# One phase for all rounded matmul operands: the second class of SBUF start addresses is given up

## The chip, the cores and the metric

The kernel runs on one core of one Trainium2 chip. The metric is the device time of one execution in microseconds (us); the figure of a kernel is the median of its runs. The core's engines are TensorE (matmuls, "PE" in the profile, with its weight loads shown apart as "PEld"), VectorE (DVE), ScalarE (ACT), GpSimd (POOL), and SyncE, from whose queue (SPq) nearly all transfers from HBM are issued. Every operand of a matmul lies in SBUF: 128 partitions, with one byte address per tensor that is the same in all partitions. This case is about that address, taken modulo 512.

## The reference, cut to what matters

Two blocks of two layers each work on 256 tokens of width 2048, in float32. The first block is a state-space layer and a latent-attention layer, each with a layer norm behind it; the second is a gated MLP and a stick-breaking attention layer, with RMS norms. Nearly all arithmetic is in products of activations with weight matrices that are read once from HBM:

```
x = ssd_mixer:  x @ w_in (2048 x 10304) -> conv, chunked scan, gate, norm -> @ w_out (4096 x 2048)
x = dsa_mixer:  x @ w_in (2048 x 4944) -> c_q, c_kv, index, gate
                c_q @ w_uq, @ w_idx_q; per head k = w_uk c_kv, v = c_kv w_uv, softmax over the chosen keys
                (o * silu(gate)) @ w_out (4096 x 2048)
h = gmlp:       xn @ w_in (2048 x 12288) -> gelu, rms norm, token mixing, gate -> @ w_out (4096 x 2048)
h = stick:      xn @ w_in (2048 x 8192) -> q, k, v, gate; stick-breaking attention -> @ w_out (2048 x 2048)
out = rms_norm(h, final_g)
```

## The kernel before, in words

**Rounded operands in two halves.** A float32 matrix is split into a head, rounded to the type fp32r, and a rest, which is the matrix less its head, rounded again. A product of two matrices is then three matmuls in fp32r: head by head, head by rest, rest by head. ScalarE makes the head of a weight unit (`e.copy(wh, RAW)`, line 1125), VectorE its rest (line 1546), and TensorE reads both. The activations are kept in the same form: `AA` holds the transposed input of a layer (16 blocks of 128 rows, head and rest, 256 tokens each), `YY` the input of an output projection (32 such blocks), `CQ` and `CK` the normed low-rank queries and keys.

**Units and slots.** The weights come in 822 units of up to 128 x 1024 float32 (512 KB), in an order written out by `Plan`. Each unit is transferred into one of four `RAW` buffers, then cast and subtracted into a slot that holds head and rest, 8 KB in each partition. There are always three slots (`W0` to `W2`), and more where a stage leaves room: `WY24` and `WY28` inside `YY`, `Wx7`, and the spares `WA`, `WB`, `WC` around the output projections. `Plan.slots` assigns them; addresses play no part in it.

**Which operand moves.** A matmul has a stationary operand of 128 columns, loaded by a LDWEIGHTS of its own, and a moving operand that is streamed. In most blocks the weight is stationary and the activations move, 256 columns at a time. In the blocks of `TOKENS` (the output projections o1 to o4, and cq, v5, v7) the activation is stationary and the weight moves: 256 columns at a time in o1 to o4, 512 in the others. The profile's names give the moving operand first: `G<-AA,W` of shape 128x256 is AA streamed past a stationary weight unit, `G<-W,AA` of shape 128x512 is a weight unit streamed past a stationary piece of AA. All these matmuls are issued at line 703, and each has a weight load of its own.

**Where the operands lie.** Two constants give the start address modulo 512 of each rounded buffer:

```python
STILL, MOVING = 128, 496
LINES = {"CQ": MOVING, "CK": MOVING, "Wx7": STILL, "SPH": MOVING, "SPL": MOVING, "TGR": STILL, "ONR": STILL}
```

`place` (line 237 on) rounds an address up to the given phase. Each of the three main slots has two views, 368 bytes apart, in one piece of memory; `pair_of` takes the view `W3M` at phase 496 for units of o1 to o4, and `W3` at phase 128 for all others (names `W0m` and `W0` in the profile):

```python
        W3.append(place(f"W{i}", [P, 2 * UW], R, line=STILL))
        W3M.append(place(f"W{i}m", [P, 2 * UW], R, top[0] - 8 * UW + MOVING - STILL))
        top[0] += MOVING - STILL
    AA = place("AA", [P, 16, 2, T], R, line=MOVING)
```

`YY` with `WY24` and `WY28` and the copy `AS` of AA that v5 and v7 read as stationary for most of their units (made by SyncE's `copy_in`) lie at 128; the spares `WA`, `WB`, `WC` (function `spare`) at 496; `CQ`, `CK`, `SPH`, `SPL` at 496; `Wx7`, `TGR`, `ONR` at 128. All parts of these tensors that a matmul reads start a multiple of 512 bytes further on, so the phase of a tensor is the phase of each of its operands. Float32 tensors, used by the small matmuls and transposes between, are placed at multiples of 64 bytes with no phase of their own.

**Order of the work.** Each engine has its own program, written out in the same walk over the blocks (`walk`). The TensorE program runs a unit of matmuls, then one step of each active side task (transposes, scores, sums over partitions: tiles named `M<-...`), then the next unit. A unit waits for its rest (`rest`), a slot's next cast waits for the last matmul that reads the slot.

Of the kernel before, what the change touches and what calls it, by code (L numbers as in the profile page):

```python
# [19 lines left out]
NEG = -1.0e30  # L20
SCALE = 128.0 ** -0.5
SPANS = ((0, P), (P, 384))
STILL, MOVING = 128, 496
LINES = {"CQ": MOVING, "CK": MOVING, "Wx7": STILL, "SPH": MOVING, "SPL": MOVING, "TGR": STILL, "ONR": STILL}
GATES = ((1, 2), (3,), (4,), (5,), (6,), (7,), (), ())
LAST_COLS = ((0, 512), (512, 512), (1024, 512), (1536, 256), (1792, 256))
# [2397 lines left out]
```

How the kernel before makes its waits and increments, by code:

```python
        def fetch(u):  # L561
            s = u % NR
            if u >= NR:
                e.wait_ge(*on("rest", u - NR))
            for a0, nk, width, o, cn, src in units[u][3]:
                dst = RAW[:, s, a0:a0 + nk * width].rearrange("p (k n) -> p k n", k=nk)[:, :, o:o + cn]
                e.dma_start(dst, src).then_inc(*landed(raw_here[s], "raw", u))
            fetched[0] = u + 1
# [22 lines left out]
        def dt_task():  # L591
            for _ in range(8):
                yield
            e.wait_ge(*on("dt", "cs"))
            e.dma_start(cs_d[:, :], YT[0:64, 1, :]).then_inc(*landed(d["cs_stored"], "csd"))
            yield
# [1 line left out]
        def ssd(g):  # L598
            for _ in range(6):
                yield
            if g == 0:
                e.wait_ge(*on("csd"))
                e.wait_ge(*on("conv", ("bc", 0), 0, 3))
            else:
                e.wait_ge(*on("decay", g - 1, 1))
            e.dma_start(CSB[:, :, :], cs_d[8 * g:8 * g + 8, :].rearrange("h t -> (h t)").partition_broadcast(P)
                        ).then_inc(*landed(d["cs_landed"], "cs", g))
            yield
# [1 line left out]
        def ev_ms():  # L610
            e.wait_ge(*on("kw"))
            e.wait_ge(*on("end2", "act"))
            e.dma_start(KI[0:64, :], KW[0:64, :]).then_inc(*landed(d["ki_landed"], "ki"))
            e.dma_start(KI[64:128, :], KW[0:64, :]).then_inc(*landed(d["ki_landed"], "ki"))
            yield
# [34 lines left out]
        def copy_in(s):  # L650
            e.wait_ge(*done(("o2" if s == 1 else "o3", 4)))
            for h in range(2):
```

## Time and profile before

| | |
|---|---|
| median of 3 runs | 2435.77 us (2435.55 to 2437.74) |
| the profiled execution, span | 2435.7 us, 45481 instructions |
| PE busy | 2423.8 us (100%), 19626 matmuls |
| weight loads (PEld) busy | 2341.2 us (96%) |
| DVE / ACT / POOL busy | 1571.2 (65%) / 1243.2 (51%) / 90.5 us (4%) |
| HBM | 452.18 MB read, 187 GB/s over the span |

The span is the time from the first to the last instruction of the profiled execution. The profile gives no other time for that execution; its span is 0.07 us under the median of the runs. A matmul's own duration (some 275 ns for 256 columns) is longer than the distance between two starts, since matmuls are pipelined: the pace of the stream is read from the starts, that is from the first column of the timeline and the counts behind it. "Busy" is the union of the overlapping durations.

### The profile page before, as it was taken

The numbers are of one execution on the slowest core, as the hardware profiler recorded it, in microseconds if no ns is written. First come the engines' busy times: TensorE is split into PE (matmuls) and PEld (weight loads), VectorE is DVE, ScalarE is ACT, GpSimd is POOL, SyncE is SP. The second block draws the span as 40 slices with busy tenths as digits, with TensorE's granted clock in tenths as the row PEclk, the third lists the DMA queues.
The fourth block names the chain that finished last, engine by engine and source line by source line (L and its number), as shares of the span: only waits on it lengthen the run. The fifth ranks groups of instructions, "written<-read, shape, count | busy, mean of one in ns | idle before, by whom it ended". The sixth has DMA issues, their size and how long they took to land.

```text
span 2435.7 us, 45481 instructions
## 1 busy us (share of the span) xinstructions
PE 2423.8 (100%) x19626; PEld 2341.2 (96%) x19626; DVE 1571.2 (65%) x2109; ACT 1243.2 (51%) x1426; POOL 90.5 (4%) x68
## 2 busy tenths in 40 slices
PE   9999999999999999999999999999999999999998
PEld 9999999999999999999988899999999999999998
DVE  6778878866577776666575555655655555555556
ACT  5445665554454565554464444544544445455453
POOL 0001000110021000000000000000000000000002
PEclk9999999999999999999999999999999999999999
DMA  7665656657755645546757666666555576555645
GB/s 238 198 196 180 210 180 187 185 174 236 232 175 174 199 150 165 152 150 231 232 185 244 190 203 198 187 186 197 180 190 186 190 233 208 184 171 178 188 161 182
DMA packets 267434, 467.93 MB, mean 192 GB/s; under 512 B 18955, under 2 KB 70497, under 8 KB 265313
## 3 DMA queue, kind: packets, MB, share of 16 engines
q1 hardware_dynamic: 267233, 465.02, 60.9%
q8 instruction: 155, 2.54, 0.4%
q14 instruction: 46, 0.38, 0.1%
HBM read 452.18 MB, written 4.26 MB: 187 GB/s over the span
## 4 chain that ended last, share of the span: by engine, by line
PE 98%; DVE 1%; ACT 0%; issue 0%; DMA 0%; SPq 0%; ACTq 0%
PE G L703 91%; PE M L703 5%; PE M L716 1%; DMA RAW<-in_ssd_w_in 0%; DVE W2m L1546 0%; DVE W0m L1546 0%; DVE E L1639 0%; ACT W0m L1125 0%; DVE E L1680 0%; DVE SZ L1708 0%; DVE E L1641 0%; ACT L1205 0%; DVE W L1546 0%; DVE W1m L1546 0%; ACT YY L1131 0%
## 5 line engine op out<-in xcount | busy, mean ns | idle before, releaser
L703 PE MATMUL G<-AA,W 128*128 128x256 f32 x7908 | 942.6, 277 | 1.1 <-DVE W L1546 1.0
L703 PEld LDWEIGHTS G<-AA,W 128*128 128x128 f32 x7908 | 917.9, 188 | 7.3 <-issue 4.1
L1546 DVE TENSOR_TENSOR W<-RAW,W 128x1024 fp32r<-128x1024 f32 x446 | 557.4, 1251 | 370.6 <-ACT W L1125 369.4
L1125 ACT CAST W<-RAW 128x1024 fp32r<-128x1024 f32 x446 | 464.8, 1047 | 467.7 <-PE G L703 457.8
L703 PE MATMUL G<-AA,WY 128*128 128x256 f32 x2508 | 305.3, 278 | 0.0
L703 PEld LDWEIGHTS G<-AA,WY 128*128 128x128 f32 x2508 | 293.2, 188 | 2.5 <-issue 2.2
L1546 DVE TENSOR_TENSOR WY<-RAW,WY 128x1024 fp32r<-128x1024 f32 (+1 forms) x112 | 140.8, 1259 | 74.9 <-ACT WY L1125 74.9
L703 PE MATMUL G<-W0m,YY 128*128 128x256 f32 x1512 | 183.8, 276 | 1.0 <-DVE W0m L1546 1.0
L703 PE MATMUL G<-W1m,YY 128*128 128x256 f32 x1512 | 182.9, 276 | 0.1
L703 PE MATMUL G<-W,YY 128*128 128x512 f32 x792 | 181.3, 389 | 0.0
L703 PE MATMUL G<-W2m,YY 128*128 128x256 f32 x1488 | 180.5, 276 | 0.0
L703 PEld LDWEIGHTS G<-W0m,YY 128*128 128x128 f32 x1512 | 176.9, 188 | 1.8 <-DVE W0m L1546 1.5
L703 PEld LDWEIGHTS G<-W,YY 128*128 128x128 f32 x792 | 148.4, 188 | 30.8
L703 PEld LDWEIGHTS G<-W1m,YY 128*128 128x128 f32 x1512 | 176.6, 188 | 0.5 <-DVE W1m L1546 0.3
L703 PEld LDWEIGHTS G<-W2m,YY 128*128 128x128 f32 x1488 | 174.0, 188 | 0.4 <-issue 0.2
L1125 ACT CAST WY<-RAW 128x1024 fp32r<-128x1024 f32 (+1 forms) x112 | 116.2, 1043 | 101.2 <-PE G L703 100.1
L1546 DVE TENSOR_TENSOR W1m<-RAW,W1m 128x1024 fp32r<-128x1024 f32 x63 | 77.2, 1225 | 74.3 <-ACT W1m L1125 74.2
L1546 DVE TENSOR_TENSOR W0m<-RAW,W0m 128x1024 fp32r<-128x1024 f32 x63 | 78.4, 1244 | 68.4 <-ACT W0m L1125 68.3
L1546 DVE TENSOR_TENSOR W2m<-RAW,W2m 128x1024 fp32r<-128x1024 f32 x62 | 76.9, 1241 | 67.7 <-ACT W2m L1125 67.4
L1125 ACT CAST W0m<-RAW 128x1024 fp32r<-128x1024 f32 x63 | 66.2, 1051 | 80.8 <-PE G L703 80.7
L1125 ACT CAST W1m<-RAW 128x1024 fp32r<-128x1024 f32 x63 | 66.1, 1050 | 80.5 <-PE G L703 78.1
L1125 ACT CAST W2m<-RAW 128x1024 fp32r<-128x1024 f32 x62 | 65.2, 1052 | 79.6 <-PE G L703 78.3
(306 smaller groups left out, 2398.0 us busy)
## 6 DMA issues: line engine op xcount, KB each, us to landing
RAW<-in_a_w_in SPq DMA_DIRECT2D x192, 512.0 KB, 3.8
RAW<-in_ssd_w_in SPq DMA_DIRECT2D x160, 512.0 KB, 4.4
RAW<-in_b_w_in SPq DMA_DIRECT2D x128, 512.0 KB, 4.1
RAW<-in_dsa_w_in SPq DMA_DIRECT2D x72, 512.0 KB, 3.6
RAW<-in_ssd_w_out SPq DMA_DIRECT2D x64, 512.0 KB, 4.6
RAW<-in_dsa_w_out SPq DMA_DIRECT2D x64, 512.0 KB, 4.1
RAW<-in_a_w_out SPq DMA_DIRECT2D x64, 512.0 KB, 3.6
RAW<-in_b_w_out SPq DMA_DIRECT2D x32, 512.0 KB, 3.7
```

The lines of the kernel that those rows point to most:

```text
L703: return e.matmul(o, l, r, start=start, stop=stop, skip_group_check=True)
L716: return e.transpose(o, i, idn)
L1125: e.copy(wh[:, 0:n], RAW[:, v % NR, 0:n]).then_inc(*up(cast_done, "cast", v))
L1546: e.tensor_tensor(wl[:, 0:n], RAW[:, v % NR, 0:n], wh[:, 0:n].bitcast(F), ALU.subtract).then_inc(*up(rest_done, "rest", v))
```

## The change

Both constants become 128. Nothing else in the code is edited.

```diff
--- before.py
+++ after.py
@@ -20,7 +20,7 @@
-STILL, MOVING = 128, 496
+STILL, MOVING = 128, 128
 LINES = {"CQ": MOVING, "CK": MOVING, "Wx7": STILL, "SPH": MOVING, "SPL": MOVING, "TGR": STILL, "ONR": STILL}
```

What follows from it: `AA`, `CQ`, `CK`, `SPH`, `SPL`, the spares and the units of o1 to o4 in the main slots start at phase 128. The two views `W3` and `W3M` of a slot fall together. The slots lose the 368 bytes between the views, so AA starts 1392 bytes lower, and the small float32 tensors behind it (`ident`, `ones` and so on) move down with it, by 1408 bytes. YY and what is laid out behind it keep their phases; the float32 tensors behind `CK` and `CQ` in the attention stage change theirs by 128 bytes. The instructions, their number, their order, the units, the slots, the transfers and all waits stay as they are.

## Rows read from the trace of the kernel before

**Rows 1.** The page, part 1, and the granted clock in 40 slices.

```profile
PE 2423.8 (100%) x19626; PEld 2341.2 (96%) x19626; DVE 1571.2 (65%) x2109; ACT 1243.2 (51%) x1426; POOL 90.5 (4%) x68
PEclk9999999999999999999999999999999999999999
```

**Rows 2.** The page, part 4: the chain of work that ended last.

```profile
PE 98%; DVE 1%; ACT 0%; issue 0%; DMA 0%; SPq 0%; ACTq 0%
```

**Rows 3.** Groups by shape, PE: the twelve rounded groups of 256 moving columns, less one.

```profile
L703 PE MATMUL G<-AA,W 128*128 128x256 f32 x7908 | 942.6, 277 | 1.1 <-DVE W L1546 1.0
L703 PE MATMUL G<-AA,WY 128*128 128x256 f32 x2508 | 305.3, 278 | 0.0
L703 PE MATMUL G<-W0m,YY 128*128 128x256 f32 x1512 | 183.8, 276 | 1.0 <-DVE W0m L1546 1.0
L703 PE MATMUL G<-W1m,YY 128*128 128x256 f32 x1512 | 182.9, 276 | 0.1
L703 PE MATMUL G<-W2m,YY 128*128 128x256 f32 x1488 | 180.5, 276 | 0.0
L703 PE MATMUL G<-AA,Wx 128*128 128x256 f32 x528 | 63.9, 276 | 0.0
L703 PE MATMUL G<-CQ,W 128*128 128x256 f32 x456 | 54.3, 277 | 0.0
L703 PE MATMUL G<-WA,YY 128*128 128x256 f32 x408 | 47.7, 275 | 0.0
L703 PE MATMUL G<-WB,YY 128*128 128x256 f32 x408 | 47.6, 275 | 0.0
L703 PE MATMUL G<-CK,W 128*128 128x256 f32 x192 | 23.6, 278 | 0.0
L703 PE MATMUL G<-WC,YY 128*128 128x256 f32 x48 | 5.9, 275 | 0.0
```

**Rows 4.** The same view: groups of 512 moving columns with the stationary operand at 496.

```profile
L703 PE MATMUL G<-W,AA 128*128 128x512 f32 x240 | 57.0, 394 | 0.0
L703 PE MATMUL G<-WY,CK 128*128 128x512 f32 x72 | 18.2, 401 | 0.0
L703 PE MATMUL G<-WB,AA 128*128 128x512 f32 x60 | 15.6, 403 | 0.0
L703 PE MATMUL G<-WA,AA 128*128 128x512 f32 x60 | 15.6, 403 | 0.0
L703 PE MATMUL G<-W,CK 128*128 128x512 f32 x24 | 6.1, 400 | 0.0
```

**Rows 5.** Timeline of PE, 2030 to 2047 us: start, duration, operands, count (moving 496, stationary 128).

```profile
2036.67 2.88 PE L703 MATMUL G<-AA,Wx 128*128 128x256 f32 x24
2039.39 5.60 PE L703 MATMUL G<-AA,W 128*128 128x256 f32 x48
```

**Rows 6.** Timeline of PE, 2108 to 2122 us (512 columns, moving 128, stationary 128).

```profile
2108.49 2.88 PE L703 MATMUL G<-Wx,YY 128*128 128x512 f32 x12
2111.21 8.32 PE L703 MATMUL G<-W,YY 128*128 128x512 f32 x36
```

**Rows 7.** Timeline of PE, 696 to 713 us (AA at 496 as stationary).

```profile
697.00 8.56 PE L703 MATMUL G<-W,AA 128*128 128x512 f32 x36
705.40 2.94 PE L703 MATMUL G<-WA,AA 128*128 128x512 f32 x12
708.17 4.32 PE L703 MATMUL G<-AA,W 128*128 128x256 f32 x36
712.33 0.93 PE L716 MATMUL M<-ident,QKB 128*128 128x128 f32 x7
```

**Rows 8.** Timeline of PE, 708.28 to 709.60 us: the first 13 matmuls behind the change of operands.

```profile
708.17 1.71 PE L703 MATMUL G<-AA,W 128*128 128x256 f32 x13
```

**Rows 9.** Windows: each engine's busy us (and instructions) in two steady stretches, granted clock, DMA.

```profile
60.00:120.00 60.00, 60.00 (x531) 60.00 (x531) 45.51 (x73) 25.17 (x25) 0.00 (x0) 1.00 0.67 199
600.00:660.00 60.00, 60.00 (x532) 60.00 (x531) 34.22 (x31) 26.21 (x26) 0.00 (x0) 1.00 0.76 242
```

## The prediction

> **What bounds the kernel now.** I read the page's first part, then the chain of waits, then the groups by shape, then the timeline of TensorE. Part 1 has TensorE busy for 2423.8 of 2435.7 us, its weight loads for 96%, VectorE for 65%, ScalarE for 51%, and the granted clock at its upper level (2.4 GHz) in all slices [rows 1]. The chain of what ended last is 98% PE and 0% DMA [rows 2]. So whatever changes the distance between two matmuls changes the time one for one, and nothing else does while the others are slack.
>
> Busy time does not give that distance, since matmuls overlap in the pipeline; starts do. In the timeline 24 matmuls of 256 columns, with AA (496) moving and a unit at 128 stationary, start at 2036.67 and the next row at 2039.39: 2.72 us / 24 = 113.3 ns each [rows 5]. At 2.4 GHz that is 272 cycles for 256 columns, 16 over. The stretches 60 to 120 and 600 to 660 us (AA, and the weights at 496, as moving) hold 531 and 532 matmuls in 60 us, 113 ns each, with a DMA share of 0.67 and 0.76 and different load on VectorE and ScalarE [rows 9]: the pace depends on none of these. With 512 columns, both operands at 128, 12 matmuls take 2.72 us: 226.7 ns, 544 cycles, 32 over [rows 6].
>
> The start addresses do matter, and the trace has the experiment. With AA (496) stationary and the weights still moving from 128, 36 matmuls of 512 columns take 705.40 - 697.00 = 8.40 us, 233.3 ns each: 6.6 ns, or 16 cycles, more than with a stationary operand at 128 [rows 6, 7]. With both at 496 it is 2.77 us / 12 = 230.8 ns, 4.1 more [rows 7]. The same operands also start slowly: behind a change of shape or a group of small matmuls the first dozen matmuls of 256 columns run slower and then fall into 113.3. In the case shown, 13 of them cover 1.71 us; without the 0.28 us of the last one's own length that is 1.43 / 12 = 119.2 ns [rows 3, 8]. So a weight load and a matmul that read at once can cost each other some 4 to 7 ns, and at 113.3 they do not: it is a pattern in time that two streams must fall into, and their start addresses are part of it.
>
> **The change part by part.**
>
> *Stationary operands that go from 496 to 128.* These are AA where v5, v7 and cq read it, and CK in the value units. 240 + 72 + 24 = 336 matmuls [rows 4] lose 233.3 - 226.7 = 6.6 ns, 2.2 us; the 60 + 60 with WA and WB moving lose 4.1 ns, 0.5 us. Together 2.7 us less, 0.1% of the span. This part I take as sure, since the pair that they become, 128 and 128 with 512 columns, is the one of rows 6.
>
> *Moving operands that go from 496 to 128, 256 columns.* These are 16,992 matmuls: the eleven groups shown and one of 24 more [rows 3]. At 113.3 ns they are 1925 us, four fifths of the kernel. The pair 128 moving, 128 stationary, 256 columns is nowhere in the trace, so I bound it by its neighbours. Lower bound: half of 226.7, that is 113.3, no change. It holds if the 32 cycles over in a matmul of 512 columns are spread evenly over its columns. A pace under 113.3 I exclude, as no rounded group of the trace shows fewer cycles per column than 17/16. Upper bound: +6.7, that is 120.0 ns. It holds if the 32 cycles all arise in the first 256 columns, while the weight load is reading beside the matmul: then 256 columns take 256 + 32 = 288 cycles. That is also about what the stationary operand's phase was worth above (6.6 ns). Between the ends lie the two measured costs of a pair that has not found the pattern: 4.1 ns for the pair with one phase on both sides that is at 496, and 119.2 - 113.3 = 5.9 ns in a slow start. I take their mean, 5.0 ns, and so 118.3 ns as the pace. My reason for the inside of the range and not its lower end is that rows 6 has something that this pair will not have. With 512 columns the load of 128 columns reads during only half of the matmul, so a slip has time to be made good before the next load; with 256 columns the loads are busy 96% of the time and every slip meets the next one. The sum: 16,992 x 5.0 ns = 85.0 us. Of this the matmuls of the slow starts have had their part: I count 1705 distances of 115 to 130 ns among these matmuls' starts, as in the stretch of rows 8, 9.0 us above 113.3 in sum. Net +76.0 us.
>
> *The rest.* CQ, SPH and SPL are moving operands too (CQ is counted in the groups of 256 columns; SPH and SPL are 64 matmuls and at 5 ns each 0.3 us, which I leave out). The small float32 tensors move by 1408 bytes, QKB and its neighbours change phase by 128: the float32 matmuls are 1226 of 19,626, and if each changed by 1 ns it would be 1.2 us either way; I take 0. ScalarE and VectorE write the same bytes elsewhere; they are 51% and 65% busy [rows 1], and a slower TensorE gives them more room, so nothing of theirs comes onto the path. The slots, their releases and the transfers keep their order; with slower matmuls each transfer has more time.
>
> *A rule that speaks otherwise.* The Trainium skill ("TensorE: Matmul & The Clock Gate", under "Step-by-step: what each phase is for") says that the weight load and the moving operand have independent read ports, so that loading the next weights steals nothing from the running matmul. By that rule no address would matter, the sum would be 0, and the time 2436. The trace does not agree as far as the stationary operand goes: its phase alone changes the distance of matmuls of 512 columns by 6.6 ns [rows 6, 7], though the load has twice the time that it needs. The chance that the rule holds for the moving operand all the same lies within that of the rival named next.
>
> **Sum.** 2435.7 + 76.0 - 2.7 = 2509 us for the profiled execution, and the median of the runs is 0.07 us from that execution's span, so 2509 for the median too: 3% slower.
>
> **The rivals.**
>
> *The pattern is kept (2433 us).* The pair at 128 and 128 runs at 113.3 with 256 columns as it does with 512, and only the 2.7 us are gained: 2435.7 - 2.7 = 2433.0, within the measurement of no change. For it: the exact half of 226.7, and the same relation of the two streams' starts in both. Against it: the slack of the 512 columns, and 230.8 at 496 and 496, which shows that one phase on both sides is not by itself enough.
>
> *The full step (2538 us).* Each matmul of 256 columns takes 288 cycles. 16,992 x 6.7 = 113.8 us, less 9.0 and 2.7: 2538. With the slower starts unchanged on top it is 2547. For it: whole steps of 16 cycles are what both 233.3 and 226.7 are made of. Against it: 230.8 is not a whole step.
>
> *The slower starts vanish (2424 us).* This is the other side, faster. Place: the first dozen matmuls behind each group of small ones. With the same phase on both sides the streams could be in the pattern from the first matmul on; then 9.0 us go besides the 2.7, 2435.7 - 11.7 = 2424. It decides as long as the steady pace rises by less than 0.7 ns, at which 16,992 matmuls eat up the 11.7 us. Against it: in rows 7 and 8 the slow start follows on a stretch whose operands were both at 496, so one phase did not protect.
>
> *The change does nothing*, because the addresses were equal modulo a smaller size already: 496 and 128 are 112 and 0 modulo 128, and 48 and 0 modulo 64, so they differ, and the stationary operand's 6.6 ns shows that the difference is felt. I give it no chance of its own; its time is that of no change.
>
> **How the numbers follow.** The forecast, a lasting cost of 4 to 6 ns, has a chance of 0.40, with its own range of 2490 to 2525. The full step has 0.20, the kept pattern 0.30, the faster start 0.08, and 0.02 are left for costs above the upper bound. The range 2431 to 2550 takes in the first three with their bounds and leaves out about 0.10. A difference of 0.2%, 5 us, is about what a measurement of this kernel can tell from none. The kept pattern is within it (2.7 us), so: faster 0.08, same 0.30, slower 0.62.
>
> **What would show it.** In the profile of the changed kernel the steady stretch 60 to 120 us should hold 60 / 0.1183 = 507 matmuls where it held 531; 531 says the pattern is kept, 500 the full step. The stretches of v5 and v7 with AA stationary should run at 226.7 as in rows 6. The mean duration of a matmul of 256 columns should go from 275 to about 280 ns. If the time is up but the steady distance is still 113.3, the loss is in longer slow starts and my mechanism is in the wrong place. The forecast is wrong if the time is under 2470 us. VectorE and ScalarE should keep the mean durations of their instructions; if these change, the addresses act on them too, which nothing here allows for.

## The result, and the profile after

The changed kernel takes 2532.01 us (median of 4 runs, 2531.77 to 2532.92) against 2436.36 us of the kernel before in the same comparison: a ratio of 1.0396, 95% interval 1.0383 to 1.0408. It is 4% slower. The forecast was 2509 with a range of 2431 to 2550, and a cost of 5.0 ns for each matmul of 256 columns; the cost is 6.7. The measured time is outside 2490 to 2525, the forecast's own narrower range, and 6 us from the rival called the full step.

Part 1 of the page after, with the granted clock, answers to [rows 1]. The instructions are the same, and TensorE's busy time is up by 96.1 us, that of its weight loads by 98.9; no other engine's is.

```profile
span 2530.5 us, 45481 instructions
PE 2519.9 (100%) x19626; PEld 2440.1 (96%) x19626; DVE 1568.8 (62%) x2109; ACT 1241.4 (49%) x1426; POOL 89.2 (4%) x68
PEclk9999999999999999999999999999999999999999
```

Two steady stretches of the changed kernel (busy us and counts of PE, PEld, DVE, ACT, POOL; granted clock; DMA share; GB/s) answer to [rows 9]. Where 531 and 532 matmuls stood in 60 us there are 502 and 503.

```profile
60.00:120.00 60.00, 60.00 (x502) 60.00 (x501) 43.60 (x70) 23.69 (x23) 0.00 (x0) 1.00 0.65 187
600.00:660.00 60.00, 60.00 (x503) 60.00 (x502) 35.27 (x33) 25.50 (x25) 0.00 (x0) 1.00 0.77 245
```

The timeline of PE in the changed kernel (start, duration, operands, count) gives the pace. In the first output projection 12 matmuls take 702.23 - 700.79 = 1.44 us, 120.0 ns or 288 cycles each. The block that answers to [rows 7] follows: AA, now at 128, as the stationary operand of 512 columns takes 8.16 / 36 = 226.7 ns where it took 233.3, and 2.72 / 12 = 226.7 where the weights came from WA and it took 230.8.

```profile
700.79 1.60 PE L703 MATMUL G<-W1m,YY 128*128 128x256 f32 x12
702.23 1.60 PE L703 MATMUL G<-W0m,YY 128*128 128x256 f32 x12
703.67 1.60 PE L703 MATMUL G<-WA,YY 128*128 128x256 f32 x12
...
725.45 8.32 PE L703 MATMUL G<-W,AA 128*128 128x512 f32 x36
733.61 2.88 PE L703 MATMUL G<-WA,AA 128*128 128x512 f32 x12
736.33 4.48 PE L703 MATMUL G<-AA,W 128*128 128x256 f32 x36
```

Groups by shape answer to [rows 3] and [rows 4]: the mean duration of a matmul of 256 columns goes from 277 to 284 ns, whichever tensor moves; that of 512 columns with AA stationary falls from 394 to 389, and with W and YY it was 389 already.

```profile
L703 PE MATMUL G<-AA,W 128*128 128x256 f32 x7908 | 986.9, 284 | 1.0 <-DVE W L1546 0.9
L703 PE MATMUL G<-W0m,YY 128*128 128x256 f32 x1512 | 193.1, 284 | 0.4 <-DVE W0m L1546 0.4
L703 PE MATMUL G<-W,AA 128*128 128x512 f32 x240 | 55.5, 389 | 0.0
```

The distances from the start of each matmul to the next one's, summed by kind over both traces, account for the whole difference of the spans, 2530.5 - 2435.7 = 94.8 us:

| distances behind | before, us | after, us | difference |
|---|---|---|---|
| 16,992 rounded matmuls of 256 columns | 1961.0 | 2060.2 | +99.2 |
| 1344 rounded matmuls of 512 columns | 309.8 | 307.4 | -2.4 |
| 1290 other matmuls | 156.2 | 154.2 | -2.0 |

Of the first kind, 15,728 distances are exactly 120 ns after, and 15,032 were 113 or 114 before.

### The profile page after: what moved, and what is told of

Same layout as the page of the kernel before. It is cut to its first block, busy times and chain, and to the rows that moved or that the text cites. A ratio compares the mean times of both kernels' runs of the same rounds, so it can differ in the third digit from the quotient of the medians.

```text
span 2530.5 us, 45481 instructions
## 1 busy us (share of the span) xinstructions
PE 2519.9 (100%) x19626; PEld 2440.1 (96%) x19626; DVE 1568.8 (62%) x2109; ACT 1241.4 (49%) x1426; POOL 89.2 (4%) x68
## 4 chain that ended last, share of the span: by engine, by line
PE 98%; DVE 1%; SPq 0%; ACT 0%; DMA 0%; issue 0%; ACTq 0%
PE G L703 92%; PE M L703 5%; PE M L716 1%; DMA RAW<-in_ssd_w_in 0%; SPq L582 0%; SPq L578 0%; DVE W0m L1546 0%; ACT W0m L1125 0%; SPq L567 0%; DVE E L1680 0%; ACT L1192 0%; DVE W L1546 0%; DVE W1m L1546 0%; DVE W2m L1546 0%; ACT W L1125 0%
## 5 line engine op out<-in xcount | busy, mean ns | idle before, releaser
L703 PE MATMUL G<-AA,W 128*128 128x256 f32 x7908 | 986.9, 284 | 1.0 <-DVE W L1546 0.9
L703 PEld LDWEIGHTS G<-AA,W 128*128 128x128 f32 x7908 | 961.0, 192 | 7.2 <-issue 3.7
L1546 DVE TENSOR_TENSOR W<-RAW,W 128x1024 fp32r<-128x1024 f32 x446 | 551.5, 1238 | 407.7 <-ACT W L1125 406.5
L703 PE MATMUL G<-AA,WY 128*128 128x256 f32 x2508 | 319.5, 285 | 0.0
L703 PEld LDWEIGHTS G<-AA,WY 128*128 128x128 f32 x2508 | 307.0, 192 | 2.5 <-issue 1.9
L703 PE MATMUL G<-W0m,YY 128*128 128x256 f32 x1512 | 193.1, 284 | 0.4 <-DVE W0m L1546 0.4
L703 PE MATMUL G<-W1m,YY 128*128 128x256 f32 x1512 | 192.7, 283 | 0.0
L703 PE MATMUL G<-W2m,YY 128*128 128x256 f32 x1488 | 190.0, 284 | 0.0
L703 PEld LDWEIGHTS G<-W0m,YY 128*128 128x128 f32 x1512 | 186.1, 192 | 0.9 <-DVE W0m L1546 0.6
L703 PEld LDWEIGHTS G<-W1m,YY 128*128 128x128 f32 x1512 | 186.2, 192 | 0.2 <-issue 0.2
L703 PEld LDWEIGHTS G<-W2m,YY 128*128 128x128 f32 x1488 | 183.3, 192 | 0.3 <-issue 0.2
L1125 ACT CAST W1m<-RAW 128x1024 fp32r<-128x1024 f32 x63 | 65.9, 1047 | 88.8 <-PE G L703 86.9
```

The costliest lines, as they stand in the source:

```text
L703: return e.matmul(o, l, r, start=start, stop=stop, skip_group_check=True)
L1125: e.copy(wh[:, 0:n], RAW[:, v % NR, 0:n]).then_inc(*up(cast_done, "cast", v))
L1546: e.tensor_tensor(wl[:, 0:n], RAW[:, v % NR, 0:n], wh[:, 0:n].bitcast(F), ALU.subtract).then_inc(*up(rest_done, "rest", v))
```

## The experiments

Each is compared with the kernel before on the same chip where it is timed. A "pair" is (moving phase, stationary phase), each the start address modulo 256 or 512. The "floor" is the lowest steady pace seen: 113.3 ns for 256 columns and 226.7 for 512. A "break" is a matmul of another kind, or a few, put in front of a stream of equal ones. Each bench is one profiled execution, so a pace read in it is one reading, from one start.

**1. A map of phases.** The bench's core; each pair has its own tensors, named by phase (`M128m` moving, `S192s` stationary):

```python
    for mp, sp, cols, scols, n in configs:
        m, s = made["M", mp], made["S", sp]
        for i in range(n):
            o = G[0:scols, k % 8, 0:cols]
            a, b = 256 * (i % 2) if cols <= 256 else 0, 128 * ((i // 2) % 2)
            last = e.matmul(o, s[:, b:b + scols], m[:, a:a + cols], start=True, stop=True, skip_group_check=True)
...
PH = list(range(0, 512, 16))
...
CONFIGS += [(mp, sp, 256, 128, 40) for mp in (496, 128) for sp in PH]
```

> Leaves out the whole computation: it copies x into SBUF tensors that start at each multiple of 16 modulo 512 (M... as moving, S... as stationary operand), runs rounded matmuls back to back for pairs of them, and stores x. Read from the starts of the matmuls. Theory 1 (the weight load and the moving stream read at the same time and cost each other cycles by where both start): with 128 stationary columns the pair moving 128, stationary 128 takes 120.0 ns at 256 columns and 226.7 at 512, so the 32 extra cycles lie in the first 256 columns, and 320 columns take 146.7, 384 take 173.3, 448 take 200.0 ns; and with fewer stationary columns (96, 64, 32) at 256 moving columns the extra cycles shrink in proportion to the load. Theory 2 (the moving operand's own start address costs the cycles, whatever the load does): the extra stays with 32 stationary columns, and at 256 columns the pace depends on the moving phase alone, 113.3 at 496 and 120.0 at 128 for every stationary phase. Theory 3 (only the distance of the two phases matters): the pace is the same along equal differences, so moving 368 with stationary 0 takes 113.3, and 496 with 496 takes 120.0.

Its timeline with 256 columns and the stationary operand at 128: from 64, 40 matmuls in 4.56 us (114.0 ns, the first few are slower); from 128, 4.79 us (119.8).

```profile
63.89 4.72 PE L42 MATMUL G<-M64m,S128s 128*128 128x256 f32 x40
68.45 4.93 PE L42 MATMUL G<-M80m,S128s 128*128 128x256 f32 x40
73.22 4.90 PE L42 MATMUL G<-M96m,S128s 128*128 128x256 f32 x40
77.95 4.85 PE L42 MATMUL G<-M112m,S128s 128*128 128x256 f32 x40
82.64 4.95 PE L42 MATMUL G<-M128m,S128s 128*128 128x256 f32 x40
87.43 2.78 PE L42 MATMUL G<-M144m,S128s 128*128 128x256 f32 x22
```

And with 128 moving and the stationary operand changed: 192 takes 4.54 us for 40, 113.5 ns each.

```profile
852.75 4.87 PE L42 MATMUL G<-M128m,S176s 128*128 128x256 f32 x40
857.46 4.70 PE L42 MATMUL G<-M128m,S192s 128*128 128x256 f32 x40
862.00 4.92 PE L42 MATMUL G<-M128m,S208s 128*128 128x256 f32 x40
```

So theory 2 falls: with the moving operand at 128 the pace goes from 113.3 to 120.1 ns with the stationary phase alone. Theory 3 falls in its plain form: moving both by 128 changes nothing (368 with 0 runs at 113.3), but (496, 496) ran at 118.3 and (128, 128) at 120.0. Nearly everything repeats with 256 bytes, with exceptions such as (0, 496) at 117.3 against (256, 496) at 120.0 and (128, 112) at 117.3 against (128, 368) at 120.0; and one pair, (128, 0), was run twice and took 118.7 and 120.1. Experiment 7 shows what can be behind such cases. No pair of the map went under 113.3. Theory 1 is half right, since the pair decides, but its account of where the extra cycles lie fails. The groups of (128, 128) by shape (the second factor of `128*32` is the number of stationary columns):

```profile
L42 PE MATMUL G<-M128m,S128s 128*128 128x512 f32 x32 | 7.5, 390 | 0.0
L42 PE MATMUL G<-M128m,S128s 128*128 128x448 f32 x32 | 6.8, 368 | 0.0
L42 PE MATMUL G<-M128m,S128s 128*128 128x384 f32 x32 | 5.7, 334 | 0.0
L42 PE MATMUL G<-M128m,S128s 128*128 128x320 f32 x32 | 4.9, 310 | 0.0
L42 PE MATMUL G<-M128m,S128s 128*32 128x256 f32 x32 | 3.9, 280 | 0.0
L42 PE MATMUL G<-M128m,S128s 128*128 128x192 f32 x32 | 3.8, 275 | 0.0
L42 PE MATMUL G<-M128m,S128s 128*128 128x128 f32 x32 | 3.7, 273 | 0.0
```

Less the last one's own length the first four are, over 31 distances, about 229, 207, 173 and 148 ns; their second halves, where the pace is steady, are 226.6, 206.6, 173.3 and 146.7. With 320 and 384 columns it is 32 extra cycles as theory 1 has it, but with 448 it is 48 (200.0 was expected). With 32 stationary columns the load is a quarter and the extra is not: 117.8 ns, 27 cycles over 256; with 64 it is 113.4. The extra does depend on the load, but not in proportion to it. Two more readings of this bench belong here. With 128 and with 192 moving columns the pace is the same, 111.6 to 111.7 ns, for all four pairs tried, (128, 128), (496, 128), (128, 496) and (496, 496): below some 268 cycles a matmul with a load of 128 columns did not come. And a shorter load does not take 256 columns under the floor: with 32 stationary columns (496, 128) and (128, 496) run at 113.4.

**2 and 3. Half of the change undone.** `AA = place("AA", ..., line=496)` alone; then the views `W3M` and the spares alone at 496.

> Only AA goes back to 496, all else stays at 128. The cost is per matmul: 7908 + 2508 + 528 = 10,944 matmuls of 256 columns with AA moving go from 120.0 to 113.3 ns, 73.0 us less than 2532; the stationary reads of AA with 512 columns go back to 233.3 (252 of them, +1.7 us) and 120 with WA and WB moving come to 233.3 too (+0.8). So 2461 us. If instead some shared cause (the moved float32 tensors, the slots lying closer) made the loss, it stays near 2532.

> Only the weights as moving operands go back to 496 (the views of the main slots in o1 to o4, and the spares), AA, CQ and CK stay at 128. 3 x some 1500 + 408 + 408 + 48 = 5376 matmuls of 256 columns go from 120.0 to 113.3 ns, 35.8 us less than 2532: 2496 us. The spares at 496 with AA stationary at 128 and 512 columns are a pair the trace has not shown; by theory 1 with 16 extra cycles in all they take 220.0 ns each (120 matmuls, 0.8 us less), by an even spread 226.7.

With AA back: 2472.29 us (ratio to before 1.0147, interval 1.0130 to 1.0164), 11 us more than expected. With the moving weights back: 2499.86 us (1.0262, 1.0247 to 1.0277), 4 us more. They take back 59.7 and 32.2 us of 95.7, which adds up to within 4 us. The same stretches, AA back first, moving weights back second: each half has its stage at 532 matmuls in 60 us and leaves the other at 502.

```profile
60.00:120.00 60.00, 60.00 (x532) 60.00 (x531) 45.50 (x71) 26.08 (x25) 0.00 (x0) 1.00 0.69 196
600.00:660.00 60.00, 60.00 (x502) 60.00 (x502) 33.54 (x31) 25.82 (x25) 0.00 (x0) 1.00 0.72 229
```

```profile
60.00:120.00 60.00, 60.00 (x502) 60.00 (x501) 43.59 (x70) 23.67 (x23) 0.00 (x0) 1.00 0.63 182
600.00:660.00 60.00, 60.00 (x532) 60.00 (x531) 37.96 (x36) 26.99 (x26) 0.00 (x0) 1.00 0.77 256
```

So the cost is per matmul and local. AA gives back less than the 73 us expected, mostly because (496, 128) brings its slow starts back and (128, 128) has none: over the 10,751 distances below 130 ns behind a matmul with AA moving the mean is 114.03, not 113.3, which is 7.5 us. The spares at 496 with AA at 128 and 512 columns, on which theory 1 and an even spread differed, met neither's figure (220.0 and 226.7): their mean distance without the breaks is 231 ns.

**4. The full map modulo 256.** The same bench, `for sp in PH for mp in PH` with `PH = 0, 16, ... 240`, for 256 and for 512 columns, two float32 matmuls ahead of each pair.

> Leaves out the whole computation, as the first bench did. Each pair of a moving and a stationary phase (multiples of 16 modulo 256, with 256 and with 512 moving columns) runs behind two float32 matmuls that break the stream. If the rule 'moving = stationary - 64 modulo 256' is what the first bench showed, all 16 pairs of that difference run 256 columns at 113.3 ns, and the start behind the break is short for them (under 3 slow matmuls); moving 240 with stationary 128 runs at 113.3 behind some 10 slow matmuls, moving 128 with 128 at 120.0. If the good pairs are single cases and not a rule, some of the 16 are above 113.3. With 512 columns at least the pairs (128, 128), (112, 128) and (128, 112) should be at 226.7, and the map says whether that is the difference 0 at every phase.

With 256 columns 22 of 256 pairs run at 113.3 to 113.4 over the second half of their matmuls (a 23rd, (112, 0), gets there later) and none below; most lie from 116.6 to 120.1, the worst at 123.3. With 512 columns 34 pairs run at 226.7. They are not the same pairs: (128, 128) is among the 34 and the slowest kind among the 256-column ones; of difference 0 only 0, 32, 64, 128 and 160 reach 226.7. Of the 34 only three, (112, 48), (112, 176) and (240, 176), are at the floor with 256 columns too. Of the 16 pairs with a difference of -64, the rule that was expected, 11 ran at 113.3 to 113.4, among them all eight with a stationary phase that is an odd multiple of 16; the other five, (192, 0), (224, 32), (0, 64), (32, 96) and (160, 224), ran at 117.8. The rule as it was put does not hold.

**5. The same phase again, 256 bytes lower.** `STILL, MOVING = 128, 240`.

> MOVING = 240, 256 bytes under the 496 of before, STILL = 128. If only the address modulo 256 counts, as the bench has it (moving 64 like 320, 240 like 496, 128 like 384), the time is that of the kernel before, 2436 us, and 4% under that of the kernel after. If 512 is the period, or the gain at 496 is special to it, it lies above 2440.

2435.70 us, ratio 0.9998 (0.9989 to 1.0008). For this pair the period is 256; 496 is nothing special. The buffers behind the slots lie elsewhere than in the kernel before, so this also speaks against their places in memory as the cause.

**6. The moving operands left at 128, the stationary ones moved.** `STILL, MOVING = 192, 128` (with the distance of the two views of a slot taken modulo 512).

> MOVING stays 128 and STILL goes to 192: the moving operands stay where the changed kernel has them. If the moving address itself is what costs (theory 2), nothing is gained, 2532 us. If the pair counts, the matmuls of 256 columns go back to 113.3 ns, and with short starts: 2532 - 99 (the difference of the two traces in these matmuls) - up to 9 for the slow starts = 2424 to 2433. The matmuls of 512 columns (192 with 192, and 192 moving with AA at 128) are a pair not yet seen: between 226.7 and 234 ns for 1344, so 0 to 9 us more: 2424 to 2442 us.

2468.34 us, ratio 1.0126 (1.0111 to 1.0142). 64 us are won back without touching the moving address, so the pair counts; but it is 26 to 44 us more than expected. The trace shows why: the pair runs at two paces, and keeps to one for long, 113.3 for most of 26 to 193 us and 117.8 for most of 1107 to 1458 us. Timeline of this kernel near 63 us (5.44 / 48 = 113.3 ns) and near 600 us (2.83 / 24 = 117.9):

```profile
63.11 5.60 PE L703 MATMUL G<-AA,WY 128*128 128x256 f32 x48
68.55 5.72 PE L703 MATMUL G<-AA,W 128*128 128x256 f32 x49
```

```profile
599.91 2.99 PE L703 MATMUL G<-WA,YY 128*128 128x256 f32 x24
602.74 2.99 PE L703 MATMUL G<-W2m,YY 128*128 128x256 f32 x24
605.57 2.99 PE L703 MATMUL G<-W1m,YY 128*128 128x256 f32 x24
```

**7. Many starts.** Thirteen pairs, each behind 24 different breaks:

```python
BREAKS = [("f", c, n) for c in (128, 256, 64, 16) for n in (1, 2, 3)]        # float32, c columns, n of them
BREAKS += [("r", c, n) for c in (128, 192, 320, 384, 512, 64) for n in (1, 2)]  # rounded
```

> Leaves out the whole computation. Thirteen pairs of phases, each behind 24 different breaks (float32 matmuls of 16 to 256 columns, rounded ones of 64 to 512), 24 matmuls of 256 columns behind each. In the kernel with 128 moving and 192 stationary, a pair that ran at 113.3 in the bench, half the matmuls ran at 117.8 in a repeated pattern. If a pair has more than one lasting pattern, and the timing at the start picks one, (128, 192) ends at 113.3 behind some of the breaks and at 117.8 behind others, while (240, 128), the pair of the kernel before, ends at 113.3 behind all, and (128, 128) at 120.0 behind all. If each pair has one pace, all 24 ends agree and the loss in the kernel has another cause.

Timeline for (128, 192) behind three of them; the pace of the last nine distances of these groups of 24 is 117.8, 113.3 and 117.8 ns. The whole groups last 3.07, 2.99 and 3.04 us.

```profile
212.09 3.07 PE L50 MATMUL G<-M128m,S192s 128*128 128x256 f32 x24
215.00 0.74 PE L42 MATMUL G<-SRC 128*128 128x16 f32 x6
215.59 2.99 PE L50 MATMUL G<-M128m,S192s 128*128 128x256 f32 x24
218.41 0.22 PE L45 MATMUL G<-M128m,S192s 128*128 128x128 f32 x1
218.47 3.04 PE L50 MATMUL G<-M128m,S192s 128*128 128x256 f32 x24
```

(128, 192) ended at 113.3 behind 14 breaks and at 117.8 behind 10; (64, 128) behind 15, (96, 160) behind 18, (112, 48) behind 12. (240, 128) ended at 113.3 behind all but the very first break, right behind the bench's idle start, where the distances were 213.3 ns; (128, 128) behind none. (16, 80), (208, 96), (48, 192) and (176, 64) ended there behind all 24. Without the first distance behind a break, the 22 others of a group of (16, 80) sum to 19 ns over 22 x 113.3 on average, those of the three others to 40 to 44. The remaining three, (240, 224), (208, 192) and (240, 176), each at the floor in the map, ended there behind only 3, 4 and 10 breaks. So a pair can have more than one lasting pattern, and what goes before picks one: of the twelve pairs here that had the floor in the map, seven did not hold it.

**8. A pair with a short start.** `STILL, MOVING = 160, 96`.

> STILL = 160, MOVING = 96 in the whole kernel: the pair (96, 160) ran at 113.3 in the bench with an excess of 3 ns at the start (240 with 128: 50 ns), 512 columns at (160, 160) at 226.7, and at 160 moving with 96 stationary at 228.9 (before: 233.3). If the start always finds 113.3: some 8 us of slow starts and 336 x 4.4 = 1.5 us less than before, 2426 us, and this kernel beats both. If the pair has a second lasting pattern like (128, 192), whose difference is the same, between 2445 and 2500 us.

2442.99 us, ratio 1.0031 (1.0019 to 1.0043): slower than before by 0.3%, and 2 us under the low end of the second case. In its trace 3905 of the 16,992 distances lie between 115 and 130 ns, against 1705 before; of its 192 long stretches of these matmuls (20 and more in a row) 40 end at about 118 ns. The pair has the second pattern.

**9. Choosing pairs.** The same breaks, other pairs, four of them with 512 columns:

> Leaves out the whole computation. The same 24 breaks, now for eleven pairs of 256 columns and four of 512, to choose a set for the whole kernel: AA at 16 and the weight slots at 80 were the only pair of the last bench that ended at 113.3 behind all breaks with a shorter start (excess 19 ns behind a break against 40 and more), and with 512 columns 80 moving and 16 stationary ran at 226.7. If the difference of -64 made that, (208, 16), (48, 112), (112, 176), (240, 48), (144, 208) and (80, 144) do the same; if each pair is a case of its own, some of them end at 117 to 118 behind part of the breaks. (240, 128) should end at 113.3 behind all again.

All ten other pairs ended at 113.3 behind all 24 breaks. The eight whose stationary phase is an odd multiple of 16 and whose moving phase is 64 less, (16, 80), (208, 16), (48, 112), (112, 176), (240, 48), (144, 208), (80, 144) and (176, 240), did so with 18 to 23 ns over, counted as above. The three of that difference with a stationary phase of an even multiple of 16 tried in experiment 7 did not hold. With 512 columns (80, 16) was at 226.7 behind all 22 breaks that could be told apart from it. The three others with 512 columns did not hold their floor: (128, 128), the pair of rows 6, kept it behind 15 of the 24 breaks, (80, 112) behind 17 and (80, 176) behind 14.

**10. The whole kernel on such pairs, and 11. one phase for all at 240.**

The set has AA, CQ, CK and YY at 16, the slots at 80 and the weights of o1 to o4 as moving operands at 208; WY24 and WY28 lie 64 bytes further on inside YY. The edit against the changed kernel, without the unchanged lines between:

```diff
-STILL, MOVING = 128, 128
+STILL, MOVING, ACROSS_O = 80, 16, 208
-            off = (top[0] + 63) // 64 * 64 if line is None else top[0] + (line - top[0]) % 512
+            off = (top[0] + 63) // 64 * 64 if line is None else top[0] + (line - top[0]) % 256
-        W3M.append(place(f"W{i}m", [P, 2 * UW], R, top[0] - 8 * UW + MOVING - STILL))
-        top[0] += MOVING - STILL
+        W3M.append(place(f"W{i}m", [P, 2 * UW], R, top[0] - 8 * UW + ACROSS_O - STILL))
+        top[0] += ACROSS_O - STILL
-    YY = place("YY", [P, 32, 2, T], R, line=STILL)
+    YY = place("YY", [P, 32, 2, T], R, line=MOVING)
-    WY = {24: place("WY24", [P, 2 * UW], R, y_at + 24 * 8 * T),
-          28: place("WY28", [P, 2 * UW], R, y_at + 28 * 8 * T)}
+    top[0] += STILL - MOVING
+    WY = {24: place("WY24", [P, 2 * UW], R, y_at + 24 * 8 * T + STILL - MOVING),
+          28: place("WY28", [P, 2 * UW], R, y_at + 28 * 8 * T + STILL - MOVING)}
-            o += (MOVING - o) % 512
+            o += (ACROSS_O - o) % 512
```

The other kernel is the changed one with `STILL, MOVING = 240, 240`.

> The whole kernel with phases chosen from the maps: weight slots as stationary (and as moving with 512 columns) at 80, AA, CQ, CK, SPH, SPL and YY at 16, the weights of o1 to o4 as moving at 208. Pairs: (16, 80) and (208, 16) with 256 columns, (80, 16) with 512, each at the floor behind all 24 breaks, 113.3 and 226.7 ns. Against the kernel before: slow starts 19 to 23 ns instead of some 50 behind each of 206 interruptions, 6 us less; the 336 stationary reads of AA and CK with 512 columns at 226.7 instead of 233.3, 2.2 us, and a little at the WA and WB units: 2427 us, 0.35% faster than before. If the second lasting pattern turns up in the kernel though no break of the bench found it, over 2440.

> One phase for all, as in the changed kernel, but 240 instead of 128. The map has the pair (240, 240) at 116.7 ns with 256 columns and 229.8 with 512, against 120.0 and 226.7 at (128, 128). If the map holds in the kernel: 16,738 x (116.7 - 120.0) = -55.2 us and 1344 x 3.1 = +4.2 us from 2532: 2481 us. If equal phases cost the same wherever they lie (theory 3), 2532.

The chosen set: 2430.94 us (11 runs), ratio to before 0.998, interval 0.9971 to 0.9989. It beats both kernels, the one before by some 5 us (0.2%) and the changed one by 4%; 9 us were expected. Its trace has 1181 distances of 115 to 130 ns, 5.7 us over in sum (before: 1705 and 9.0), and 512 columns sum to 307.3 us (before 309.8). None of its 192 long stretches ends over 114.5 ns, against 40 in the kernel of experiment 8 and 95 in that of experiment 6. The block of [rows 7] in it: 8.19 / 36 = 227.5 and 2.76 / 12 = 230.0.

```profile
694.18 8.35 PE L704 MATMUL G<-W,AA 128*128 128x512 f32 x36
702.37 2.92 PE L704 MATMUL G<-WA,AA 128*128 128x512 f32 x12
705.13 4.26 PE L704 MATMUL G<-AA,W 128*128 128x256 f32 x36
```

One phase at 240: 2502.51 us, ratio 1.0277 (1.0262 to 1.0291); 30 us better than one phase at 128 (so equal phases don't cost the same everywhere), not the 51 that the map gave. In its stretch of 60 to 120 us there are 510 matmuls, 117.6 ns each, where the map's single start had 116.7; that it has more than one pattern is likely but was not tried behind several breaks.

```profile
60.00:120.00 60.00, 60.00 (x510) 60.00 (x509) 44.31 (x72) 23.96 (x23) 0.00 (x0) 1.00 0.65 187
```

## Why the prediction was right, and where its size was off

- *What bounds the kernel* held. The distances between matmuls account for all 94.8 us, and VectorE and ScalarE only got more room: the mean of VectorE's rest of a unit went from 1251 to 1238 ns and that of ScalarE's head from 1047 to 1044.
- *Stationary operands to 128*: -2.7 us forecast, -2.4 measured for all matmuls of 512 columns. The pair of rows 6 was carried over to AA and came out at 226.7 in the long stretches. In the short ones, between breaks, it did not: with CK stationary the mean distance without the breaks went from 233.6 to 229.7, with WA moving from 231.9 to 230.0. So this part was less sure than it was called, as experiment 9 shows too.
- *Moving operands to 128*: direction and place right, the size of the term too small. I took 5.0 ns, 118.3 ns as the pace; it is 6.7 ns and 120.0. That is the rival called the full step, to which I gave 0.20. Its sum, 2538, is 6 us over the 2532; the forecast is 23 under. It is the only term that was mis-sized by more than a microsecond or two. The +99.2 of the table is made up of 6.67 ns x 16,991 distances = 113.3 us, less 9.0 for the slow starts that were there, less 1.6 for distances that now lie a little under 120, less 3.4 in the distances over 130 ns. These last are the first distances behind breaks, and 15 of before at the clock's lower level (see the last section), which the changed kernel's profiled execution did not have: some 1.4 us of the difference are theirs and have nothing to do with the change.
- *Why I chose 5.0.* I averaged the 4.1 of (496, 496) and the 5.9 of a slow start, and counted it against the full step that 230.8 is not a whole number of steps of 16 cycles. Both figures belong to other pairs or to slow starts, and their mean stood for no mechanism; that it came within a quarter of the true cost is in part luck. The trace had a number for that pair, the 32 extra cycles of rows 6, and the upper bound made the right number of them. But its reason, that they "all arise in the first 256 columns", does not hold, since 448 columns have 48.
- *The slack argument* (a slip can be made good with 512 columns, not with 256) gave the right side, but the maps lend it little: 34 of 256 pairs are at the floor with 512 columns and 22 with 256, a difference of kind in the pairs more than in their number. The map gives the direction another support: of the 34 only three are at the floor with 256 columns, so a pair known from 512 columns alone was likely not to be. That a slip is made good in the slack no run shows.
- *The kept pattern* (0.30) did not come about: half of 226.7 is not the pace at 256 columns for this pair. *The slower starts vanish*: they did, as (128, 128) is at 120 nearly at once behind a break, but the pace rose far more than the 0.7 ns that the rival allowed.
- *The offset of 0.07 us* in the sum set a median beside the span of another execution. The changed kernel's profiled execution took 2531.77 us with a span of 2530.5, so 1.3 us belong there; it changes nothing above.
- *The rule that speaks otherwise.* By the Trainium skill ("SBUF — State Buffer", "Who interferes with whom") TensorE has two independent SBUF read ports and never waits on anyone. These runs do not bear out that its two streams leave each other alone: with the moving operand at 128, the stationary phase alone moves the pace from 113.5 (192) to 120.0 ns (128). Whether it is a port that they share, no run shows.

**What stays open.** Why a pair has the pattern that it has. It depends on both addresses modulo 256, on the number of moving and of stationary columns, and on the timing at the start; a matmul without its weight load was not tried, so the share of the load in the 16 cycles that every pair of 256 columns has over 256 is not known; a load of a quarter of the columns left them as they were (113.4 ns).

## What to carry to other kernels

When TensorE runs rounded float32 matmuls back to back, each with its own weight load, look at the distance between starts and not at busy time: if it is over 113.3 ns for 256 columns at 2.4 GHz, try other start addresses for the pair. A stationary operand at an odd multiple of 16 bytes and a moving one 64 bytes below, modulo 256, held the floor behind every start tried here, for all eight such pairs; two of them were tried in a whole kernel. It is a rule for these shapes, 256 moving and 128 stationary columns; with 512 columns other pairs are good. Test a pair in the kernel or behind many different breaks, since a pace measured once from one start can be one of several.

## What the runs showed of the hardware that was not expected

- The whole kernel's time repeats with 256 bytes of address (2435.70 us with 240 for 496), and so do nearly all pairs of the first bench.
- One pair can have two lasting paces, 113.3 and 117.8 ns, in the same kernel, each for a hundred microseconds and more in places (experiment 6).
- At the clock's lower level the pair of the kernel before, (496, 128), has no extra cycles. In the trace of the kernel before the granted clock is 0.50, that is 1.2 GHz, from 9.4 to 12.6 us, behind a start in which TensorE was partly idle (2.81 us busy of the 4 from 4 to 8 us), and 15 matmuls of 256 columns take 3.20 us: 213.3 ns, exactly 256 cycles. Just behind, at 1.00, it takes 3.20 us for 30 (small ones among them). No other pair was seen at the lower level.

```profile
9.40:12.60 3.20, 3.20 (x15) 3.20 (x16) 1.69 (x2) 0.65 (x1) 0.00 (x0) 0.50 1.05 405
12.80:16.00 3.20, 3.20 (x30) 3.20 (x30) 0.86 (x1) 1.94 (x4) 0.00 (x0) 1.00 1.01 291
```

The first group of experiment 7 ran at the same 213.3 ns, though the view of its stretch (22 to 26 us) gives a granted clock of 1.00; there the lower level is inferred from the pace and not shown.

- With 128 columns to load for each matmul, 128 and 192 moving columns took the same 111.6 to 111.7 ns (experiment 1).
- At 2.4 GHz no rounded pair ran 256 columns steadily in under 272 cycles or 512 in under 544, whatever the phases.
